# Down-weight loads of a 32-expert layer moved from SyncE's queue to ScalarE's

## The chip, the core and the metric

The kernel runs on one NeuronCore of one Trainium2 chip. The metric is the device time of one execution in microseconds. A profiled execution has a span, from its first to its last instruction; the device time is a little longer than the span. Names of engines in the rows: PE is TensorE (PEld its weight loads), DVE is VectorE, ACT is ScalarE, POOL is GpSimd, SP is SyncE. A "q" behind a name (SPq, ACTq) is the engine's sequencer when it issues a DMA.

## What is computed

One decoder layer for 256 tokens of width 1024: an attention mixer, a layer norm, a mixture of experts, a layer norm. Everything is float32. The change touches the mixture of experts only:

```python
def moe_ffn(h, ...):                      # 256 tokens, 32 experts, top 4
    logits = xt @ router_w + router_b
    top_logit, top_e = lax.top_k(logits, TOP_K)
    top_w = softmax(top_logit)
    # for each expert e, over the tokens xb that chose it, with weights w:
    gu = xb @ w_gu[e] + b_gu[e]           # 1024 x 2048: 8 MB of weights
    gate = minimum(gu[:, :1024], 7.0)
    up = clip(gu[:, 1024:], -7.0, 7.0)
    act = gate * sigmoid(1.702 * gate) * (up + 1.0)
    y = act @ w_dn[e] + b_dn[e]           # 1024 x 1024: 4 MB of weights
    out[tokens] += y * w
```

## The kernel before

The engines run five instruction streams, written by hand, and they order themselves with semaphores. The attention part and the router take the first 212 us of the span. After that come the 32 experts, in a rolled loop over 15 pairs (`Fori(0, PAIRS - 1)`) and a written-out last pair. An expert has 64 token slots; tokens beyond 64 go through `extra_blocks`, a conditional loop of 32-slot blocks behind the expert's down projection. In these inputs two experts have one extra block each, both with an odd number (experts 1 and 15).

Weights in SBUF. There are two gate-up slots of 8 MB (`gu_slot[0]`, `gu_slot[1]`), for even and odd experts, and one down slot of 4 MB (`dn_slot`). Each load is cut into four chunks: a gate-up chunk is 2 MB in 256 rows of 8 KB, a down chunk 1 MB in 256 rows of 4 KB. Every chunk has a semaphore of its own (`s_gul`, `s_dnl`), for which TensorE waits ahead of the chunk's matmuls.

TensorE's order (lines 1124 to 1170), for a pair of experts 2i and 2i+1: `combine` of the last pair, `gate_up(1)` for expert 2i+1, two `gather`s, `down(0)` for expert 2i, transposes, `gate_up(0)` for expert 2i+2, `down(1)` for expert 2i+1, transposes. So an expert's down projection stands behind the gate-up projection of the expert after it. A gate-up chunk increments `guc` when it has been used, a down chunk `dn_used`; chunks used by extra blocks increment `xguc` and `xdnc`.

SyncE's order (lines 368 to 389): for each expert e, first the four gate-up chunks of expert e+2, each as soon as the chunk that lies in its place has been used (waits on `guc` and `xguc`, lines 374 and 375), then the four down chunks of expert e+1, each as soon as the down chunk of e in its place has been used (waits on `dn_used` and `xdnc`, lines 379 and 380). All 256 expert loads are issued by SyncE, at line 325 (gate-up) and line 330 (down). They lie in its one DMA queue in this order, and SyncE stands still at each wait.

ScalarE's order (lines 685 to 705): for each expert a `sigmoid` (line 656), for every other one two copies of gathered tokens (`slots_to_sbuf`, line 622), then `expert_output` (line 672, the copy of half of the down result out of PSUM, behind all four `dn_used` of the expert), `extra_blocks`, and `act_columns` (line 660, the copy of the transposed activations that the next `down` multiplies; for even experts TensorE also waits for it, `actT`, ahead of the next `gate_up(1)`). `combine_weights` (line 667) ends the pair.

Of the kernel before, what the change touches and what calls it, by code (L numbers as in the profile page):

```python
# [13 lines left out]
P = 128  # L14
# [3 lines left out]
KT = D // P  # L18
DH = 64
CMP_LEN, CMP_STRIDE, CMP_BLOCKS = 32, 16, 16  # L20
N_EXPERTS = 32
TOP_K = 4
PAIRS = N_EXPERTS // 2
# [6 lines left out]
DN_CHUNKS = 4  # L30
# [24 lines left out]
def hybrid_layer(nc, x, w_in, b_in, pos_k, pos_v, w1_k, w2_k, w1_v, w2_v, g_out, w_out, ln1_g, ln1_b,  # L55
                 router_w, router_b, w_gu, b_gu, w_dn, b_dn, ln2_g, ln2_b, out):
    with ExitStack() as ctx:
# [3 lines left out]
        def sem(name):  # L61
            return ctx.enter_context(nc.semaphore(name))
# [6 lines left out]
        dn_slot = reg_dn.rearrange("p (k n) -> p k n", k=KT)  # L69
# [129 lines left out]
        sp = [take(768) for _ in range(2)]  # L199
# [30 lines left out]
        s = {n: sem("s_" + n) for n in names}  # L230
        s_win = [sem(f"s_win{i}") for i in range(5)]
        s_gul = [[sem(f"s_gul{e}{c}") for c in range(GU_CHUNKS)] for e in range(2)]
        s_dnl = [[sem(f"s_dnl{e}{c}") for c in range(DN_CHUNKS)] for e in range(2)]
# [55 lines left out]
        def _(sp_):  # L289
            sp = sp_  # L290
# [29 lines left out]
            dn_v = w_dn[0].rearrange("e (k p) n -> e p k n", p=P)  # L320

            def load_gu(i, par, c):
                kk = KT // GU_CHUNKS
                src = gu_v[2 * i + par] if isinstance(i, int) else gu_v[bass.ds(2 * i + par, 1)].rearrange("e p k n -> (e p) k n")
                sp.dma_start(gu_slot[par][:, kk * c:kk * c + kk, :], src[:, kk * c:kk * c + kk, :]).then_inc(s_gul[par][c], 16)  # L325

            def load_dn(i, par, c):
                kk = KT // DN_CHUNKS
                src = dn_v[2 * i + par] if isinstance(i, int) else dn_v[bass.ds(2 * i + par, 1)].rearrange("e p k n -> (e p) k n")
                sp.dma_start(dn_slot[:, kk * c:kk * c + kk, :], src[:, kk * c:kk * c + kk, :]).then_inc(s_dnl[par][c], 16)  # L330

            def count_extra_blocks(e):

                n = sp.value_load(nx[0:1, e:e + 1] if isinstance(e, int) else nx[0:1, bass.ds(e, 1)], min_val=0, max_val=MAX_EXTRA)  # L334
                sp.reg_add(xcount, xcount, n)

            def use_by_extra_blocks(c):

                return sp.snap(sp.snap(xcount, min_val=0, max_val=96) * 4 + (c + 1), min_val=1, max_val=4 * 97)
# [22 lines left out]
                load_gu(0, 1, c)  # L362
            sp.wait_ge(s["op"], 12)
            for c in range(DN_CHUNKS):
                load_dn(0, 0, c)
            sp.wait_ge(s["routed"], 1)

            with sp.Fori(0, PAIRS - 1) as i:
                for par in range(2):

                    count_extra_blocks(2 * i + par)
                    for c in range(GU_CHUNKS):
                        xc = use_by_extra_blocks(c)
                        sp.wait_ge(s["guc"], i * (2 * GU_CHUNKS) + (par * GU_CHUNKS + c + 1))
                        sp.wait_ge(s["xguc"], xc)
                        load_gu(i + 1, par, c)
                    for c in range(DN_CHUNKS):
                        xc = use_by_extra_blocks(c)
                        sp.wait_ge(s["dn_used"], i * (2 * DN_CHUNKS) + (par * DN_CHUNKS + c + 1))
                        sp.wait_ge(s["xdnc"], xc)  # L380
                        load_dn(i + par, 1 - par, c)

            count_extra_blocks(N_EXPERTS - 2)
            for c in range(DN_CHUNKS):
                xc = use_by_extra_blocks(c)
                sp.wait_ge(s["dn_used"], (N_EXPERTS - 2) * DN_CHUNKS + c + 1)
                sp.wait_ge(s["xdnc"], xc)
                load_dn(PAIRS - 1, 1, c)


            sp.wait_ge(s["guc"], (N_EXPERTS - 1) * GU_CHUNKS)
# [93 lines left out]
        def _(act):  # L485
# [134 lines left out]
            def slots_to_sbuf(h, bank, n):  # L620
                act.wait_ge(s["ga"], n)
                act.activation(xg[:, 4 * h:4 * h + 4, :].rearrange("p k s -> p (k s)"), PB[bank][:, :], ACT.Copy)\  # L622
                   .then_inc(s["xg_ok"], 1)
# [6 lines left out]
            def extra_slots():  # L630

                act.reg_add(xcount, xcount, 1)
                xc = act.snap(xcount, min_val=1, max_val=96)
                act.wait_ge(s["xga"], xc)
                act.activation(yx[:, 0:KT * XSLOTS], PB[6][:, 0:KT * XSLOTS], ACT.Copy).then_inc(s["xxg"], 1)

            def extra_sigmoid():
                act.wait_ge(s["xgok"], act.snap(xcount, min_val=1, max_val=96))
                act.activation(act_x[0:64, :], gt[0:64, :], ACT.Sigmoid, scale=SWIGLU_ALPHA).then_inc(s["xsig"], 1)

            def extra_act_copy():
                xc = act.snap(xcount, min_val=1, max_val=96)
                act.wait_ge(s["xct"], xc)
                act.activation(CTx[:, :, :].rearrange("p b t -> p (b t)"), PB[7][:, 0:256], ACT.Copy)\
                   .then_inc(s["xctd"], 1)
                act.wait_ge(s["xat"], xc)
                act.activation(actTx[:, :, :].rearrange("p c s -> p (c s)"), PB[6][:, 0:256], ACT.Copy)\
                   .then_inc(s["xactT"], 1)

            def extra_outputs():  # L650
                act.wait_ge(s["xdnc"], act.snap(act.snap(xcount, min_val=0, max_val=96) * 4 + DN_CHUNKS, min_val=1, max_val=4 * 97))
                act.activation(yx, PB[6][:, :], ACT.Copy).then_inc(s["xyd"], 1)

            def sigmoid(n):
                act.wait_ge(s["g_ok"], n)
                act.activation(act_sb, gt, ACT.Sigmoid, scale=SWIGLU_ALPHA).then_inc(s["sig"], 1)  # L656

            def act_columns(bank, n):
                act.wait_ge(s["at"], n)
                act.activation(actT[:, :, :].rearrange("p c s -> p (c s)"), PB[bank][:, :], ACT.Copy)\  # L660
                   .then_inc(s["actT"], 1)

            def combine_weights(n):

                act.wait_ge(s["ct"], n)
                act.wait_ge(s["comb"], n)
                act.activation(CT[:, :, :].rearrange("p b t -> p (b t)"), PB[6][:, 0:256], ACT.Copy)\
                   .then_inc(s["ct_sb"], 1)

            def expert_output(e, n):  # L670
                act.wait_ge(s["dn_used"], n * DN_CHUNKS)
                act.activation(ysb[64 * e:64 * e + 64, 1, :], PB[7][64:128, :], ACT.Copy).then_inc(s["ysb_ok"], 1)  # L672

            def extra_blocks(t):
                n = act.value_load(nx[0:1, t:t + 1] if isinstance(t, int) else nx[0:1, bass.ds(t, 1)], min_val=0,
                                   max_val=MAX_EXTRA)
                with act.If(n > 0):
                    with act.Fori(0, n):
                        extra_slots()
                        extra_sigmoid()  # L680
                        extra_act_copy()
                        extra_outputs()
                act.nop()

            sigmoid(1)
            act_columns(5, 1)
            combine_weights(1)
            with act.Fori(0, PAIRS - 1) as i:
                sigmoid(2 * i + 2)
                slots_to_sbuf(0, 6, 2 * i + 3)  # L690
                slots_to_sbuf(1, 4, 2 * i + 4)
                expert_output(0, 2 * i + 1)
                extra_blocks(2 * i)
                act_columns(6, 2 * i + 2)
                sigmoid(2 * i + 3)
                expert_output(1, 2 * i + 2)
                extra_blocks(2 * i + 1)
                act_columns(5, 2 * i + 3)
                combine_weights(i + 2)
            sigmoid(N_EXPERTS)  # L700
            expert_output(0, N_EXPERTS - 1)
            extra_blocks(N_EXPERTS - 2)
            act_columns(6, N_EXPERTS)
            expert_output(1, N_EXPERTS)
            extra_blocks(N_EXPERTS - 1)
# [461 lines left out]
        def _(dve):  # L1167
# [141 lines left out]
            def add_square(i):  # L1309
                kind, r = o_order[i]  # L1310
                if r > 0:
                    dve.wait_ge(s["oscaled"], i + 1)
                    a = ssq[:, {"nsa": 0, "fox": 1, "sb": 2}[kind], :]
                    tt(a, a, sq, ALU.add).then_inc(s["ssq_acc"], 1)
                    dve.wait_ge(s["ssq_acc"], sum(1 for _, q in o_order[:i + 1] if q > 0))
# [301 lines left out]
```

## Time and profile before

| | us |
|---|---|
| median of 3 runs | 1245.11 |
| lowest and highest | 1243.04 and 1245.42 |
| profiled execution, device time | 1245.07 |
| its span | 1243.3 |
| TensorE busy | 1115.8 |
| ScalarE busy | 146.3 |
| moved by the DMA engines | 426.18 MB |

The profiled execution's device time is 1.8 us above its span, and equal to the median within 0.04 us. The page divides the span into 40 slices of 31.1 us: slices 1 to 7 are attention and router, slice 8 on the experts. Times below are from the span's start. A busy time of TensorE is not a measure of its peak, since the ends of matmuls are modelled.

### The profile page before, as it was taken

Reading aid. Unit: us, or ns where it says so; the run is one execution under the profiler, and the core shown is the slowest. Engines: PE = TensorE matmul, PEld = TensorE weight load, DVE = VectorE, ACT = ScalarE, POOL = GpSimd, SP = SyncE. Lnnn points to the kernel's source line nnn. Section 1 sums busy time; section 2 is a strip of 40 time slices with the busy share of each in tenths; the row PEclk is TensorE's granted clock in tenths of the full one; section 3 lists DMA queues with packets and bytes.
Section 4 is the critical chain, followed back from the end, with each engine's and each line's share of the span. In section 5 each row is a group of like instructions: output and inputs, shape, how many; then the busy total and the mean of one; then the engine's idle time right before and its main releaser. Section 6 shows DMA issues by size and latency. Waiting matters only on the chain.

```text
span 1243.3 us, 14596 instructions
## 1 busy us (share of the span) xinstructions
PE 1115.8 (90%) x5388; PEld 489.2 (39%) x5389; DVE 266.8 (21%) x767; ACT 146.3 (12%) x309; POOL 29.7 (2%) x52
## 2 busy tenths in 40 slices
PE   7999796998899999999999978999999999999983
PEld 6677445334243333333333333434333332323321
DVE  2353535111112111120211111111212111111113
ACT  2043311100000110000100001000010010100000
POOL 2000410000000000000000000000000000000000
PEclk9999896997999999999999998999999999999997
DMA  9400849630999999999999957999999999999992
GB/s 315 180 1 1 269 196 395 273 137 2 408 418 418 418 418 418 419 418 418 418 418 418 418 243 314 418 418 418 418 418 418 418 419 418 418 418 418 418 414 119
DMA packets 80386, 426.18 MB, mean 343 GB/s; under 512 B 6009, under 2 KB 7594, under 8 KB 47562
## 3 DMA queue, kind: packets, MB, share of 16 engines
q1 hardware_dynamic: 79834, 425.37, 84.7%
q10 hardware_dynamic: 528, 0.48, 0.1%
q8 instruction: 16, 0.26, 0.1%
q14 instruction: 8, 0.07, 0.0%
HBM read 424.78 MB, written 1.05 MB: 343 GB/s over the span
## 4 chain that ended last, share of the span: by engine, by line
PE 49%; DMA 25%; SPq 18%; DVE 3%; issue 3%; ACT 1%; POOL 0%; DVEq 0%; POOLq 0%; ACTq 0%
PE PB L713 47%; DMA WB<-in_w_gate_up_dram 22%; SPq L330 11%; SPq L325 6%; DMA WB<-in_w_down_dram 3%; PE PB L1044 0%; DMA X<-in_x_dram 0%; SPq L334 0%; DVE S L1391 0%; PE PB L720 0%; DVE S L1520 0%; POOL K L476 0%; DVE WB L1285 0%; PE PB L803 0%; DVE S L1497 0%
## 5 line engine op out<-in xcount | busy, mean ns | idle before, releaser
L713 PE MATMUL PB<-WB,S 128*64 128x512 f32 (+5 forms) x3472 | 770.5, 596 | 60.6 <-DMA WB<-in_w_gate_up_dram 54.3
L713 PEld LDWEIGHTS PB<-WB,S 128*64 128x64 f32 (+2 forms) x3472 | 253.2, 140 | 541.7 <-issue 413.4
L1494 DVE TENSOR_SCALAR S<-PB 128x512 f32<-128x512 f32 (+1 forms) x34 | 23.5, 691 | 617.2 <-PE PB L713 617.2
L713 PE MATMUL PB<-S 128*64 128x512 f32 (+5 forms) x464 | 138.2, 580 | 4.7 <-issue 2.3
L656 ACT ACTIVATE S<-S 128x512 f32<-128x512 f32 x32 | 20.2, 630 | 568.7 <-DVE S L1494 568.7
L713 PE MATMUL PB<-S,X 128*128 128x128 f32 (+1 forms) x576 | 76.9, 295 | 9.3 <-DVE S L1520 8.0
L713 PEld LDWEIGHTS PB<-S,X 128*128 128x128 f32 x576 | 73.6, 211 | 23.7 <-issue 21.9
L713 PEld LDWEIGHTS PB<-S 128*64 128x64 f32 (+4 forms) x464 | 53.0, 167 | 74.4 <-issue 67.4
L1538 DVE COPY S<-PB 64x512 f32<-64x512 f32 x32 | 21.9, 684 | 197.6 <-PE PB L713 197.6
L713 PE MATMUL PB<-S,WB 128*128 128x256 f32 (+2 forms) x336 | 63.2, 388 | 0.4 <-ACT S L496 0.4
L713 PEld LDWEIGHTS PB<-S,WB 128*128 128x128 f32 (+1 forms) x336 | 49.1, 177 | 12.4 <-issue 2.1
L713 PE MATMUL PB<-WB 128*32 128x128 f32 (+7 forms) x260 | 44.6, 361 | 5.2 <-DVE WB L1358 3.3
L672 ACT ACTIVATE S<-PB 64x512 f32<-64x512 f32 x32 | 19.0, 594 | 194.9 <-PE PB L713 194.9
L713 PEld LDWEIGHTS PB<-WB 128*64 128x64 f32 (+2 forms) x260 | 27.4, 152 | 18.7 <-issue 13.7
L480 POOL TENSOR_TENSOR K<-K 128x1 f32<-128x1 f32 x2 | 3.0, 1512 | 1041.6 <-DVE K L1413 1041.6
L1044 PEld LDWEIGHTS PB<-K,S 128*128 128x128 f32 x128 | 13.4, 140 | 30.8 <-issue 27.0
L1044 PE MATMUL PB<-K,S 128*128 128x128 f32 x128 | 21.0, 287 | 4.8 <-DVE S L1500 2.8
L1497 DVE SCALAR_TENSOR_TENSOR S<-S 128x512 f32<-128x512 f32 (+1 forms) x34 | 23.5, 691 | 1.2
L1500 DVE TENSOR_TENSOR S<-S 128x512 f32<-128x512 f32 (+1 forms) x34 | 23.5, 691 | 1.2
L1495 DVE TENSOR_SCALAR S<-PB 128x512 f32<-128x512 f32 (+1 forms) x34 | 23.1, 681 | 0.1
L622 ACT ACTIVATE S<-PB 128x512 f32<-128x512 f32 x32 | 19.1, 597 | 32.9 <-PE PB L713 32.9
L1469 DVE TENSOR_SCALAR S<-K 128x64 f32<-128x64 f32 x68 | 16.9, 249 | 20.6 <-PE PB L1049 19.1
(198 smaller groups left out, 338.0 us busy)
## 6 DMA issues: line engine op xcount, KB each, us to landing
WB<-in_w_gate_up_dram SPq DMA_DIRECT2D x128, 2048.0 KB, 22.8
WB<-in_w_down_dram SPq DMA_DIRECT2D x128, 1024.0 KB, 22.9
WB<-in_w_in_dram SPq DMA_DIRECT2D x1, 3088.0 KB, 16.0
WB<-in_w_in_dram SPq DMA_DIRECT2D x1, 3072.0 KB, 20.7
WB<-in_w_in_dram SPq DMA_DIRECT2D x1, 2144.0 KB, 10.8
WB<-in_w_in_dram SPq DMA_DIRECT2D x1, 2048.0 KB, 15.8
WB<-in_w_out_dram SPq DMA_DIRECT2D x2, 1024.0 KB, 10.3
WB<-in_w_out_dram SPq DMA_DIRECT2D x1, 2048.0 KB, 16.8
```

The lines of the kernel that those rows point to most:

```text
L325: sp.dma_start(gu_slot[par][:, kk * c:kk * c + kk, :], src[:, kk * c:kk * c + kk, :]).then_inc(s_gul[par][c], 16)
L330: sp.dma_start(dn_slot[:, kk * c:kk * c + kk, :], src[:, kk * c:kk * c + kk, :]).then_inc(s_dnl[par][c], 16)
L622: act.activation(xg[:, 4 * h:4 * h + 4, :].rearrange("p k s -> p (k s)"), PB[bank][:, :], ACT.Copy)\
L656: act.activation(act_sb, gt, ACT.Sigmoid, scale=SWIGLU_ALPHA).then_inc(s["sig"], 1)
L672: act.activation(ysb[64 * e:64 * e + 64, 1, :], PB[7][64:128, :], ACT.Copy).then_inc(s["ysb_ok"], 1)
L713: return mm_(o, l, r, start=start, stop=stop, skip_group_check=True)
L1044: ins = tr(PB[bank][:, P * c:P * c + P], act_sb[:, P * c:P * c + P], ident)
L1494: ts(g, gate, LIMIT, None, ALU.min).then_inc(s[g_ok], 1)
L1495: ts(u, up, LIMIT, -LIMIT, ALU.min, ALU.max).then_inc(s[clip], 1)
L1497: stt(u, u, 1.0, g, ALU.add, ALU.mult).then_inc(s[upg], 1)
L1500: tt(a, u, a, ALU.mult).then_inc(s[done], 1)
L1538: cp(ysb[64 * e:64 * e + 64, 0, :], PB[7][0:64, :]).then_inc(s["ysb_dv"], 1)
```

## The change

SyncE issues only the first expert's down weights and all gate-up weights. The four down chunks of every later expert are issued by ScalarE, together, behind `expert_output` and `extra_blocks` of the expert before, and so behind the waits for all of that expert's down chunks; the waits on `dn_used` and `xdnc` chunk by chunk are gone. In ScalarE's stream `act_columns` comes behind the four issues. SyncE's gate-up loads keep their waits on `guc` and `xguc` and their order.

```diff
-            def load_dn(i, par, c):
+            def load_first_dn(c):
                 kk = KT // DN_CHUNKS
-                src = dn_v[2 * i + par] if isinstance(i, int) else ...
-                sp.dma_start(dn_slot[:, kk * c:kk * c + kk, :], src[...]).then_inc(s_dnl[par][c], 16)
+                sp.dma_start(dn_slot[:, kk * c:kk * c + kk, :], dn_v[0, :, kk * c:kk * c + kk, :]).then_inc(s_dnl[0][c], 16)
...
                         load_gu(i + 1, par, c)
-                    for c in range(DN_CHUNKS):
-                        xc = use_by_extra_blocks(c)
-                        sp.wait_ge(s["dn_used"], i * (2 * DN_CHUNKS) + (par * DN_CHUNKS + c + 1))
-                        sp.wait_ge(s["xdnc"], xc)
-                        load_dn(i + par, 1 - par, c)
...
+            def load_dn(t, par):
+                kk = KT // DN_CHUNKS
+                src = dn_v[t] if isinstance(t, int) else dn_v[bass.ds(t, 1)].rearrange("e p k n -> (e p) k n")
+                for c in range(DN_CHUNKS):
+                    act.dma_start(dn_slot[:, kk * c:kk * c + kk, :], src[:, kk * c:kk * c + kk, :]).then_inc(s_dnl[par][c], 16)
...
                 expert_output(0, 2 * i + 1)
                 extra_blocks(2 * i)
+                load_dn(2 * i + 1, 1)
                 act_columns(6, 2 * i + 2)
                 sigmoid(2 * i + 3)
                 expert_output(1, 2 * i + 2)
                 extra_blocks(2 * i + 1)
+                load_dn(2 * i + 2, 0)
                 act_columns(5, 2 * i + 3)
                 combine_weights(i + 2)
...
             extra_blocks(N_EXPERTS - 2)
+            load_dn(N_EXPERTS - 1, 1)
             act_columns(6, N_EXPERTS)
```

## Rows read from the trace of the kernel before

**Rows 1.** The page, part 2: granted TensorE clock and GB/s in 40 slices

```profile
PEclk9999896997999999999999998999999999999997
GB/s 315 180 1 1 269 196 395 273 137 2 408 418 418 418 418 418 419 418 418 418 418 418 418 243 314 418 418 418 418 418 418 418 419 418 418 418 418 418 414 119
```

**Rows 2.** The chain that ended last, by engine, and one piece of it

```profile
PE 49%; DMA 25%; SPq 18%; DVE 3%; issue 3%; ACT 1%; POOL 0%; DVEq 0%; POOLq 0%; ACTq 0%
...
456.01 27.93 DMA WB<-in_w_gate_up_dram
```

**Rows 3.** Stretches: us, busy PE PEld DVE ACT POOL (instructions), PEclk, DMA share, GB/s

```profile
329.80:382.60 52.80, 52.80 (x253) 19.92 (x251) 8.07 (x19) 4.40 (x8) 0.00 (x0) 1.00 1.02 417
...
442.00:502.00 60.00, 55.28 (x262) 20.50 (x260) 9.47 (x24) 5.22 (x9) 0.00 (x0) 1.00 1.02 418
...
329.20:737.10 407.90, 381.71 (x1806) 142.62 (x1803) 64.90 (x163) 35.96 (x62) 0.00 (x0) 1.00 1.01 414
...
770.00:1178.00 408.00, 381.69 (x1808) 142.96 (x1806) 64.89 (x163) 35.95 (x62) 0.00 (x0) 1.00 1.02 418
```

**Rows 4.** DMA issues by line: count, KB each, median us to landing

```profile
WB<-in_w_gate_up_dram SPq DMA_DIRECT2D x128, 2048.0 KB, 22.8
WB<-in_w_down_dram SPq DMA_DIRECT2D x128, 1024.0 KB, 22.9
```

**Rows 5.** Waits: engine, line, waited for: total us, times, longest

```profile
SPq L380 <- PE PB L713: 256.9, 85, 29.4
...
PE PB L713 <- DMA WB<-in_w_gate_up_dram: 54.3, 42, 1.4
...
PE PB L713 <- DMA WB<-in_w_down_dram: 2.1, 4, 0.6
```

**Rows 6.** Timeline of PE over one pair: start, us, line, operation

```profile
329.59 3.60 PE L713 MATMUL PB<-S 128*128 128x512 f32 x8
333.12 13.95 PE L713 MATMUL PB<-WB,S 128*64 128x512 f32 x64
...
352.49 7.09 PE L713 MATMUL PB<-WB,S 128*64 128x512 f32 x32
359.51 0.66 PE L1044 MATMUL PB<-K,S 128*128 128x128 f32 x4
...
375.60 7.04 PE L713 MATMUL PB<-WB,S 128*64 128x512 f32 x32
382.57 0.66 PE L1044 MATMUL PB<-K,S 128*128 128x128 f32 x4
383.06 0.38 PE L1049 MATMUL PB<-K,S 128*128 128x128 f32 x2
```

**Rows 7.** DMA packets by queue, 192.2 to 194.6 us (q1 SyncE's, q10 ScalarE's)

```profile
q1 hardware_dynamic: 40, 0.33, 61.2%
q10 hardware_dynamic: 38, 0.26, 41.5%
```

**Rows 8.** Expert loads of the whole span: issue to landing

```profile
DMA to landing us min/median/max: 5.0/22.8/27.9
```

**Rows 9.** Timeline around ScalarE's copies, and one of its own DMA issues

```profile
204.93 0.32 ACTq L614 DMA_DIRECT2D S<-in_b_down_dram x1
...
530.31 0.60 ACT L672 ACTIVATE S<-PB 64x512 f32<-64x512 f32 x1 [6.43 <-PE PB L713]
531.11 0.60 ACT L660 ACTIVATE S<-PB 128x512 f32<-128x512 f32 x1 [0.21 <-PE PB L1044]
```

**Rows 10.** Timeline of SyncE's queue in the steady part: four down chunks issued

```profile
491.33 15.20 SPq L330 DMA_DIRECT2D WB<-in_w_down_dram  x4
```

**Rows 11.** Around the extra block of expert 15: PE's timeline, then stretches as in rows 3

```profile
741.14 6.84 PE L713 MATMUL PB<-S,X 128*128 128x32 f32 x32 [3.98 <-DVE S L1520]
...
741.00:748.00 7.00, 6.84 (x32) 6.74 (x32) 0.00 (x0) 0.00 (x0) 0.00 (x0) 0.52 0.00 0
...
737.00:752.00 15.00, 10.54 (x54) 7.65 (x56) 3.21 (x14) 0.98 (x2) 0.00 (x0) 0.66 0.00 0
```

**Rows 12.** The last two down projections: stretches as in rows 3

```profile
1178.30:1207.90 29.60, 26.07 (x112) 8.52 (x110) 5.71 (x17) 2.20 (x4) 0.00 (x0) 1.00 1.02 415
1207.90:1220.10 12.20, 10.09 (x44) 2.85 (x44) 0.68 (x1) 1.19 (x2) 0.00 (x0) 1.00 0.91 359
```

More of the change, by code:

```diff
@@ L325, in load_gu @@
                 sp.dma_start(gu_slot[par][:, kk * c:kk * c + kk, :], src[:, kk * c:kk * c + kk, :]).then_inc(s_gul[par][c], 16)
-            def load_dn(i, par, c):
+            def load_first_dn(c):
                 kk = KT // DN_CHUNKS
-                src = dn_v[2 * i + par] if isinstance(i, int) else dn_v[bass.ds(2 * i + par, 1)].rearrange("e p k n -> (e p) k n")
-                sp.dma_start(dn_slot[:, kk * c:kk * c + kk, :], src[:, kk * c:kk * c + kk, :]).then_inc(s_dnl[par][c], 16)
+                sp.dma_start(dn_slot[:, kk * c:kk * c + kk, :], dn_v[0, :, kk * c:kk * c + kk, :]).then_inc(s_dnl[0][c], 16)
             def count_extra_blocks(e):
@@ L364, in _ @@
             for c in range(DN_CHUNKS):
-                load_dn(0, 0, c)
+                load_first_dn(c)
             sp.wait_ge(s["routed"], 1)
@@ L376, in _ @@
                         load_gu(i + 1, par, c)
-                    for c in range(DN_CHUNKS):
-                        xc = use_by_extra_blocks(c)
-                        sp.wait_ge(s["dn_used"], i * (2 * DN_CHUNKS) + (par * DN_CHUNKS + c + 1))
-                        sp.wait_ge(s["xdnc"], xc)
-                        load_dn(i + par, 1 - par, c)
-            count_extra_blocks(N_EXPERTS - 2)
[L384 to L388, printed above, removed]
+            count_extra_blocks(N_EXPERTS - 2)
             sp.wait_ge(s["guc"], (N_EXPERTS - 1) * GU_CHUNKS)
@@ L683, in extra_blocks @@
                 act.nop()
+            dn_v = w_dn[0].rearrange("e (k p) n -> e p k n", p=P)
+            def load_dn(t, par):
[3 more added lines that the diff above has]
+                    act.dma_start(dn_slot[:, kk * c:kk * c + kk, :], src[:, kk * c:kk * c + kk, :]).then_inc(s_dnl[par][c], 16)
             sigmoid(1)
```

## The prediction

> **What bounds the kernel now.** I read the page's slices first. From the eleventh slice on the DMA engines move 408 to 419 GB/s in every slice but the two around the extra block of expert 15 and the last two [rows 1]. The chain of waits gives TensorE 49%, DMA 25% and SyncE's queue 18% [rows 2]; the last two shares are one thing, a loaded queue, since the chain's pieces there are issues held back behind transfers, or a transfer such as the one of 27.93 us. The stretches say which engine ends last [rows 3]. From 329.8 to 382.6 us TensorE is busy for all of 52.80 us: it bounds. From 442 to 502 us it is busy for 55.28 of 60.00 us while the DMA rate is the same 418 GB/s: the transfers bound.
>
> Two floors of a pair of experts follow. Transfers: 8 gate-up chunks of 2048 KB and 8 down chunks of 1024 KB [rows 4] are 25.2 MB, at 418 GB/s 60.2 us (a gate-up chunk 5.0 us, a down chunk 2.5 us; per expert 20.1 and 10.0 us). TensorE: from the combine at 329.59 to the next one behind the transposes at 383.06 + 0.38 it is 53.8 us [rows 6]. Seven pairs lie between the two extra blocks in 407.9 us and seven behind the second in 408.0 us, 58.3 us a pair [rows 3]: the first are near TensorE's floor, working off what had been loaded ahead, the rest at the transfers' 60.2.
>
> The waits view must not mislead. SyncE waits 256.9 us for down chunks to be used [rows 5], and the gate-up loads queue behind that. But while it waits, its DMA queue is full: a load takes a median 22.8 us to land, and at least 5.0 us [rows 4, 8]. TensorE waits 54.3 us for gate-up weights, never over 1.4 us at a time, and 2.1 us for down weights [rows 5]. So the order in the one queue delivers each chunk about when it is needed, and the wait at SyncE costs nothing in the loaded stretches.
>
> **The change part by part.** (1) Taken from SyncE: 124 issues and their waits. Gate-up chunks can be issued earlier by the time SyncE stood at down waits. In loaded stretches that adds no bytes per second. In the two stops the DMA engines do fall dry (0 GB/s from 737 to 752 us [rows 11]), but there the gate-up loads wait for `xguc`, the extra block's own use of the slot, which stays. I cost the gain at nothing.
>
> (2) Added to ScalarE: 31 times four issues. The nearest rows: one issue of its own took 0.32 us, and behind the output copy at 530.31 the next copy started at 531.11 [rows 9]. I take 0.8 us from the end of `down` to the first issue and some 0.45 us for each, 1.8 us. The copy of the activations is late by that. For the next `down` it has a whole gate-up projection as cover; for `gate_up(1)` it has the combine, 3.6 us, plus 1.0 us of transposes ahead of it [rows 6]. So 1.8 us is hidden, if ScalarE's sequencer isn't held. If it is, see the third rival.
>
> (3) The down load itself starts later. Before, each chunk was issued when its place was free, 5.1 us from first to last. Now all four start behind the whole `down`. From `down`'s end to the first data it is 0.8 us to the issue, and the 5.0 us least landing less 2.5 us of transfer [rows 8], together 3.3 us; the last chunk's matmuls take 7.1 / 4 = 1.8 us [rows 6].
>
> (4) The two queues share the DMA engines. This decides. The only place where the trace shows both loaded is ScalarE's bias load at 192 us: 40 packets of SyncE's queue beside 38 of ScalarE's, 0.33 and 0.26 MB [rows 7]. The engines take packets in turn, one of each. There both were of 8 KB; a down chunk has rows of 4 KB and a gate-up chunk rows of 8 KB. If a turn is a row, down weights get one byte in three while gate-up loads are queued, and their 10.0 us become 30.1 us. The two bounds are 10.0 us (down weights served first) and 30.1 us; I take 30.1 us, the reading that is nearest to rows 7.
>
> The Trainium skill has this ("DMA: Bandwidth & Descriptors", Queues, rings and completion order): an engine goes round its queues and drains a packet from each before switching. The trace agrees for equal rows. The same page (SWDGE vs HWDGE vs iDMA) gives a packet as preferably no more than 4096 B. By that the turns would be of equal bytes, which is the first rival.
>
> (5) What a pair then takes. From one `down`'s end to the next with gate-up loads queued all the time: 3.3 + 30.1 + 1.8 = 35.2 us. TensorE's own time between the same points is 382.57 − 359.51 = 23.1 us for odd experts and 53.8 − 23.1 = 30.7 us for even ones [rows 6]. So odd experts' down weights are late by up to 12 us and even ones' by up to 4.5 us. Gate-up loads aren't queued all the time, however: in two such intervals they could move 2 × (30.1 × 2/3 + 5.1) = 50 us worth and a pair needs 40.1. They fill their slots, stop, and the down load gets the whole rate for a while. I give that relief to the even expert, which comes back to TensorE's 30.7 us: 35.2 + 30.7 = 65.9 us a pair. The other end is the transfers' 60.2 us. Above 60.2 the DMA engines fall dry for part of the pair, with both slots full and no down load issued, and this in turn speeds the next down load, so the pair settles between: I take the middle, 63.1 us.
>
> Sum: 14 pairs × 63.1 − (407.9 + 408.0) = 883.4 − 815.9 = **+67.5 us**. At the ends: 60.2 gives +27, 65.9 gives +107.
>
> (6) TensorE's clock. A wait of 3.98 us ahead of 741.14 us is followed by a stretch with a granted clock of 0.52 of 2.4 GHz, so 1.2 GHz nearly throughout, until past 748 us [rows 11]. The new waits for down chunks are of some 5 us each, so the last chunk's matmuls may take 3.5 instead of 1.8 us and the start of the next gate-up projection is slow too. Bounds 0 and 14 × 1.8 = 25 us; most lies beside waiting, so I take +5 us.
>
> (7) The tail. Before, from 1178.3 us, 29.6 + 12.2 = 41.8 us [rows 12]. After: combine 3.6, gate-up 15.6, down 7.1 and transposes 0.7, then 3.3 + 10.0 + 1.8 = 15.1 us for the last down weights, which no gate-up load shares: 42.1 us. I take 0. Before 329 us nothing is late: the load of expert 1's down weights has an empty queue and over 20 us.
>
> Total: 1245.1 + 67.5 + 5 = 1317.6; I say **1317 us**, 72 us slower. The sum is made against the profiled execution's 1245.07 us, which is the median.
>
> **The rivals.** *Turns of equal bytes.* Then a shared down load takes 20.1 us: 3.3 + 20.1 + 1.8 = 25.2 us against 23.1 and 30.7, 55.9 us a pair, under 60.2. Only the pairs that TensorE bounds today, some three in each half, lose 2.1 us each (13 us), and the stops and the tail some 4 us for loads that start later: 1262 us. For it: the skill's packet size. Against it: rows 7 count packets, and none there is split. Its own range is 1254 to 1275.
>
> *The freed gate-up queue fills dry time* (the other side). If gate-up loads could run while the DMA engines now stand dry, 737 to 752 us and a few us around it, 17 us of the loaded stretch behind it would be saved: 1228 us. It decides from the point at which a gate-up load is ready while SyncE stands at a down wait and its queue is dry. The `xguc` wait speaks against it in both stops.
>
> *ScalarE is held at its issues.* SyncE's four down issues take 15.20 us when its queue is loaded [rows 10]. If the room for issued rows is shared by both queues, ScalarE stands for as long, its activation copy comes 0.8 + 15.2 us behind `down`, the combine covers 4.6 us, and even intervals grow by 11.4 us: a pair is then between 30.7 + 11.4 + 23.1 = 65.2 and 77.3 us, 1342 to 1511 us, with 1427 in the middle. Against it: ScalarE's queue never holds more than four chunks, and its own issue took 0.32 us with SyncE's queue in use [rows 9].
>
> *Down weights served first.* Their load takes 10.0 us, nothing is late, and only the later start of (3) costs: 1245 to 1254 us.
>
> **How the numbers follow.** The forecast, 1275 to 1342 us: 0.63. Turns of equal bytes: 0.15. ScalarE held: 0.12. Down weights first: 0.04, of which 0.01 is within 0.2%. Dry time filled: 0.05. Nothing of all that happens and the time stays: 0.01. The range is 1256 to 1362 us: it leaves out the filled dry time, the unchanged time, down weights first and some two thirds of the third rival, 0.18. Faster by over 0.2% 0.05, within 0.2% 0.02, slower by over 0.2% 0.93; 0.2% is about what a measurement of this kernel can tell.
>
> **What would show it.** Down chunks issued by ScalarE land some 10 us after issue for the first and 30 us for the fourth where gate-up loads are queued; TensorE's waits for down weights grow from 2.1 us to over 100 us in total, and those for gate-up weights all but vanish; slices show less than 418 GB/s; pairs repeat at 60 to 66 us. ScalarE's four issues take about 0.4 us each, and the activation copy comes within 3 us. The prediction is wrong if in a window with both queues loaded ScalarE's queue moves half of the bytes or more, or if its issues take microseconds.

## The result and the profile after

| | before | after |
|---|---|---|
| device time, median us | 1244.07 | 1313.88 |
| lowest and highest, 4 runs each | 1242.36 and 1245.42 | 1308.61 and 1320.04 |
| profiled execution: device time, span | 1245.07, 1243.3 | 1308.61, 1306.8 |

The ratio is 1.057, with a 95% interval of 1.054 to 1.060: the change makes the kernel 70 us slower. The forecast was 1317 us. The profiled execution of after is the fastest of its four, so differences read from the two traces add up to 63.5 us, not 70. In the experiments one execution stood apart: of the thirteen of the kernel with the later start alone, one, the profiled one, took 2336.24 us; its ratio leaves it out, and no row of its trace is read.

The page of after, part 2: granted clock, share of the DMA engines and GB/s in 40 slices of 32.7 us.

```profile
PEclk9999897897988899899899979989899979998997
DMA  9300958435999999999999519999999999999742
GB/s 320 151 1 19 339 212 329 180 130 228 418 418 419 393 419 418 401 404 418 418 387 407 214 67 420 420 419 416 417 397 419 419 381 407 419 418 390 304 171 119
```

Against [rows 1] the ceiling is the same, 418 to 420 GB/s, but it no longer holds all the time: 393, 401, 387, 397, 381 stand in slices that nothing but experts fills, and the clock has dropped in many of them. The same 426.18 MB are moved.

The waits of TensorE in after (engine, line, waited for: total us, times, longest), then the issues with their median us to landing.

```profile
PE PB L714 <- DMA WB<-in_w_down_dram: 96.4, 30, 5.6
PE PB L714 <- DVE S L1521: 8.0, 2, 4.0
```

```profile
WB<-in_w_gate_up_dram SPq DMA_DIRECT2D x128, 2048.0 KB, 16.0
WB<-in_w_down_dram ACTq DMA_DIRECT2D x124, 1024.0 KB, 11.9
```

Compare [rows 5]: the 54.3 us of waits for gate-up weights are gone from the list, and 2.1 us for down weights have become 96.4 us. Gate-up weights are now early (they land in a median 16.0 us, before 22.8 us [rows 4]), down weights late. Their median landing of 11.9 us looks better than the 22.9 us of before, and misleads: a load that starts late may land soon and still be too late.

**One late down load, read through.** ScalarE's timeline behind expert 2's down projection (start, us, line, operation, in brackets the idle time before it).

```profile
360.94 0.59 ACT L661 ACTIVATE S<-PB 64x512 f32<-64x512 f32 x1 [9.84 <-PE PB L714]
361.86 2.00 ACTq L681 DMA_DIRECT2D WB<-in_w_down_dram  x4
363.90 0.60 ACT L649 ACTIVATE S<-PB 128x512 f32<-128x512 f32 x1 [2.36 <-issue]
```

The same four issues, asked one by one: KB and us from issue to landing.

```profile
WB<-in_w_down_dram ACTq DMA_DIRECT2D x1, 1024.0 KB, 11.6
WB<-in_w_down_dram ACTq DMA_DIRECT2D x1, 1024.0 KB, 18.6
WB<-in_w_down_dram ACTq DMA_DIRECT2D x1, 1024.0 KB, 25.6
WB<-in_w_down_dram ACTq DMA_DIRECT2D x1, 1024.0 KB, 32.6
```

The issues follow each other by 0.54 us and the landings by 7.5 us (7.0 + 0.54). A down chunk alone takes 2.5 us, so the down load runs at a third of the rate. TensorE, in the same time:

```profile
375.20 1.89 PE L714 MATMUL PB<-S 128*64 128x512 f32 x8
376.91 1.89 PE L714 MATMUL PB<-WB,S 128*64 128x512 f32 x8
381.08 3.30 PE L714 MATMUL PB<-WB,S 128*64 128x512 f32 x8 [2.28 <-DMA WB<-in_w_down_dram]
388.62 3.48 PE L714 MATMUL PB<-WB,S 128*64 128x512 f32 x8 [4.24 <-DMA WB<-in_w_down_dram]
396.17 3.68 PE L714 MATMUL PB<-WB,S 128*64 128x512 f32 x8 [4.07 <-DMA WB<-in_w_down_dram]
```

Its gate-up projection ends at 377 us, and three of the four down chunks are waited for. Their matmuls take 3.30 to 3.68 us where the first chunk's take 1.89: the granted clock is 1.00 of 2.4 GHz from 375 to 379 us, and 0.58, 0.55 and 0.50 in the stretches of the three. The last of them, columns as in [rows 3]:

```profile
396.10:399.80 3.70, 3.63 (x9) 0.79 (x9) 0.00 (x0) 0.00 (x0) 0.00 (x0) 0.50 1.01 421
```

The chain that ended last, over this stretch, by line:

```profile
by line: DMA WB<-in_w_down_dram 79.6%; PE PB L714 9.0%; ACTq L681 6.7%; issue 2.7%; ACTq L664 2.2%; ACTq L666 0.2%; ACT S L661 0.1%
```

A down load is released by ScalarE, lands, and lets `down` end, which releases the next. And it isn't for want of transfers that it is late: packets by queue from 362 to 400 us (packets, MB, share of the engines), at 418 GB/s in sum.

```profile
q1 hardware_dynamic: 1523, 11.70, 73.9%
q10 hardware_dynamic: 1088, 4.19, 27.6%
```

In these 38 us the gate-up queue moved 11.70 MB that TensorE couldn't use yet, while it waited for 4.19 MB in the other. These packets don't show the turns, since the down load fills only part of the 38 us. From 375 to 385 us both queues are loaded all the time:

```profile
q1 hardware_dynamic: 356, 2.79, 66.9%
q10 hardware_dynamic: 357, 1.40, 34.9%
```

As many packets from one queue as from the other, nearly every packet being one row, and so twice as many bytes of gate-up weights.

**Where the time went.** The stretches of seven pairs, as in [rows 3], and the stop behind the first of them:

```profile
327.20:764.30 437.10, 393.42 (x1805) 147.85 (x1803) 64.93 (x163) 35.95 (x62) 0.00 (x0) 0.95 0.94 386
799.10:1241.30 442.20, 394.16 (x1805) 147.05 (x1803) 64.93 (x163) 35.95 (x62) 0.00 (x0) 0.95 0.99 403
764.30:784.00 19.70, 15.24 (x90) 9.03 (x92) 3.21 (x14) 0.98 (x2) 0.00 (x0) 0.65 0.17 55
```

437.1 + 442.2 − 407.9 − 408.0 = 63.4 us, all of the difference. A pair takes 62.8 us in the mean; before it was 58.3. From one pair's weight transposes to the next pair's (L1049, after L1050) the full pairs of the first stretch took 53.7, 54.0, 59.6, 60.2, 60.2 and 60.2 us before, and take 73.4, 63.1, 67.2, 56.0, 67.9 and 55.8 us after: from the third on they alternate between some 67 and 56. The rest cancels: the time ahead of 327 us is 2 us less, the stop between the stretches 1.4 us more, the tail 0.6 us more.

### The profile page after: what moved, and what is told of

Read it like the earlier page. It is cut to its first block, busy times and chain, and to the rows that moved or that the text cites. A ratio compares the mean times of both kernels' runs of the same rounds, so it can differ in the third digit from the quotient of the medians.

```text
span 1306.8 us, 14351 instructions
## 1 busy us (share of the span) xinstructions
PE 1142.2 (87%) x5388; PEld 500.8 (38%) x5389; DVE 266.9 (20%) x767; ACT 146.3 (11%) x309; POOL 29.6 (2%) x52
## 2 busy tenths in 40 slices
DMA packets 80386, 426.18 MB, mean 326 GB/s; under 512 B 6009, under 2 KB 7594, under 8 KB 47562
## 4 chain that ended last, share of the span: by engine, by line
PE 47%; DMA 43%; DVE 3%; ACTq 3%; issue 2%; ACT 1%; SPq 0%; POOL 0%; DVEq 0%; POOLq 0%
PE PB L714 45%; DMA WB<-in_w_down_dram 42%; ACTq L681 2%; DMA WB<-in_w_in_dram 1%; ACTq L664 1%; PE PB L1045 1%; DVE S L1392 0%; DVE S L1521 0%; POOL K L465 0%; SPq L304 0%; DVE WB L1286 0%; PE PB L1050 0%; PE PB L804 0%; DVE S L1498 0%; DVE S L1501 0%
## 5 line engine op out<-in xcount | busy, mean ns | idle before, releaser
L714 PE MATMUL PB<-WB,S 128*64 128x512 f32 (+5 forms) x3472 | 792.0, 612 | 99.8 <-DMA WB<-in_w_down_dram 96.4
L714 PEld LDWEIGHTS PB<-WB,S 128*64 128x64 f32 (+2 forms) x3472 | 261.3, 143 | 587.3 <-issue 456.0
L714 PE MATMUL PB<-S 128*64 128x512 f32 (+5 forms) x464 | 141.4, 588 | 4.3 <-issue 2.3
L661 ACT ACTIVATE S<-PB 64x512 f32<-64x512 f32 x32 | 19.0, 594 | 318.3 <-PE PB L714 318.3
L649 ACT ACTIVATE S<-PB 128x512 f32<-128x512 f32 x32 | 19.1, 597 | 79.6 <-issue 71.7
L1045 PE MATMUL PB<-K,S 128*128 128x128 f32 x128 | 24.0, 317 | 2.9 <-DVE S L1501 2.8
L611 ACT ACTIVATE S<-PB 128x512 f32<-128x512 f32 x32 | 19.1, 597 | 33.0 <-PE PB L714 33.0
## 6 DMA issues: line engine op xcount, KB each, us to landing
WB<-in_w_down_dram ACTq DMA_DIRECT2D x124, 1024.0 KB, 11.9
WB<-in_w_in_dram SPq DMA_DIRECT2D x1, 3088.0 KB, 16.1
```

The costliest lines, as they stand in the source:

```text
L714: return mm_(o, l, r, start=start, stop=stop, skip_group_check=True)
L1045: ins = tr(PB[bank][:, P * c:P * c + P], act_sb[:, P * c:P * c + P], ident)
```

## The experiments

Theory A: the DMA engines serve the two queues in turn, row by row, so down rows of 4 KB beside gate-up rows of 8 KB get a third of the bytes, and that is nearly all of the loss. Theory B: the loss comes from the down loads' later start and from ScalarE's place in their path. Each experiment was timed beside the kernel before; its median is given with the ratio to those runs.

**Cutting the gate-up rows, two queues and one.** The first kernel changes the length of a row, and with it the number of issues; the second is its control with one queue.

```diff
-                sp.dma_start(gu_slot[par][:, kk * c:kk * c + kk, :], src[:, kk * c:kk * c + kk, :]).then_inc(s_gul[par][c], 16)
+                for h in range(2):
+                    sp.dma_start(gu_slot[par][:, kk * c:kk * c + kk, 1024 * h:1024 * h + 1024],
+                                 src[:, kk * c:kk * c + kk, 1024 * h:1024 * h + 1024]).then_inc(s_gul[par][c], 16)
...
-                    pe.wait_ge(s_gul[e][c], 16 * loaded)
+                    pe.wait_ge(s_gul[e][c], 32 * loaded)
```

> The changed kernel, with each gate-up chunk loaded as two halves of 1024 columns, so that its rows are 4 KB like the down rows; bytes, order and waits unchanged. Theory A (the queues take turns row by row): turns are now of equal bytes, a down chunk that shares the engines lands every 5.0 us instead of every 7.5 us, waits for down weights shrink from 96 us to under 45 us, and the time falls to about 1262 us (1250 to 1275). Theory B (the loss comes from the down loads' later start and from ScalarE in their path, not from the share): nothing about that is changed, 1305 to 1320 us.

> The control for the run above: the kernel before, all loads in SyncE's queue, with the gate-up chunks in halves of 4 KB rows. With one queue there are no turns, so theory A says as before, 1244 us, plus at most 10 us if 4 KB rows or twice as many issues cost anything. Theory B says the same. If this run is slower than 1254 us, the run above has to be read against it.

Measured: two queues 1276.35 us (1.026, 1.023 to 1.029), one queue 1263.49 us (1.017, 1.014 to 1.020). Waits for down weights fell to 49.7 us. The landings of four down chunks, issued 0.54 us apart, are now 5.1 us apart instead of 7.5:

```profile
WB<-in_w_down_dram ACTq DMA_DIRECT2D x1, 1024.0 KB, 9.4
WB<-in_w_down_dram ACTq DMA_DIRECT2D x1, 1024.0 KB, 14.0
WB<-in_w_down_dram ACTq DMA_DIRECT2D x1, 1024.0 KB, 18.6
WB<-in_w_down_dram ACTq DMA_DIRECT2D x1, 1024.0 KB, 23.2
```

Both times are above what was expected, for the same reason: halves of the 8 KB rows are moved at 410 GB/s, not 418. The stretch from 500 to 700 us of the one-queue control (columns of rows 3):

```profile
500.00:700.00 200.00, 179.56 (x830) 65.00 (x828) 30.38 (x82) 16.07 (x28) 0.00 (x0) 1.00 1.03 410
```

Against its control the split now costs 13 us, not 70. Theory B would have left it at 70: the later start and ScalarE's place are the same here.

**Quarters.** The same edit with four pieces of 512 columns: rows of 2 KB.

> The changed kernel, each gate-up chunk loaded as four quarters of 512 columns, rows of 2 KB against the down loads' 4 KB. Theory A: down weights now get two bytes in three while both queues are loaded, a shared down chunk lands every 3.8 us, a whole down load in some 18 us from issue, TensorE waits for down weights nearly nowhere but at the last expert, and the time is 1245 to 1275 us, unless 2 KB rows lower the 418 GB/s. Theory B: 1305 to 1320 us.

Measured: 1318.72 us (1.060, 1.058 to 1.063), 44 us above the range. The time alone would speak for theory B. The profile doesn't: TensorE's longest entry is another one, its waits for down weights are three, and the stretch from 500 to 700 us has a lower rate.

```profile
PE PB L716 <- DMA WB<-in_w_gate_up_dram: 106.5, 20, 8.6
PE PB L716 <- DMA WB<-in_w_down_dram: 5.8, 3, 5.3
```

```profile
500.00:700.00 200.00, 177.56 (x816) 66.25 (x814) 28.42 (x72) 15.67 (x27) 0.00 (x0) 0.94 1.04 394
```

Down weights land 3.9 us apart, as expected, and TensorE waits 5.8 us in all for them. Now gate-up weights are late, and at 394 GB/s a pair's 25.2 MB take 63.9 us, 5.6 us above the 58.3 of before; 14 pairs are 78 us, against 75 measured. The condition that I had put into the expectation (unless 2 KB rows lower the rate) is what happened. The kernel with one queue and quarters was not run, so how much the split costs at this ratio isn't known. Cut rows mix two effects, so the later kernels, from the whole rows on, avoid cutting.

**The later start alone.** One queue; SyncE waits for the whole of `down` before it issues the four down chunks.

```diff
-                        xc = use_by_extra_blocks(c)
-                        sp.wait_ge(s["dn_used"], i * (2 * DN_CHUNKS) + (par * DN_CHUNKS + c + 1))
-                        sp.wait_ge(s["xdnc"], xc)
+                        if c == 0:
+                            xc = use_by_extra_blocks(DN_CHUNKS - 1)
+                            sp.wait_ge(s["dn_used"], i * (2 * DN_CHUNKS) + (par * DN_CHUNKS + DN_CHUNKS))
+                            sp.wait_ge(s["xdnc"], xc)
                         load_dn(i + par, 1 - par, c)
...
```

> The kernel before with one part of the change alone: SyncE still issues the down loads in its one queue, but all four chunks together behind the whole down projection (and extra block) of the expert before, instead of chunk by chunk. Theory A: the queue is loaded in the steady part, so a start 5 us later costs nothing there and some 3 us at the last expert: 1244 to 1252 us. Theory B: the later start is most of the loss, 1290 us or more.

Measured: 1247.02 us (1.0026, 1.0010 to 1.0042). With one queue the start 5 us later costs 3 us of the 70, so the start alone isn't the loss. It says nothing of ScalarE's place, the other half of theory B, nor of a late start beside a second queue; against these speak the kernels in which both stay and the loss is 13 to 20 us.

**Down rows of 2 KB.** The other way round: the share made worse, with the same bytes.

```diff
-                    act.dma_start(dn_slot[:, kk * c:kk * c + kk, :], src[:, kk * c:kk * c + kk, :]).then_inc(s_dnl[par][c], 16)
+                    for h in range(2):
+                        act.dma_start(dn_slot[:, kk * c:kk * c + kk, 512 * h:512 * h + 512],
+                                      src[:, kk * c:kk * c + kk, 512 * h:512 * h + 512]).then_inc(s_dnl[par][c], 16)
...
```

> The changed kernel, each down chunk loaded as two halves of 512 columns, so that its rows are 2 KB against the gate-up loads' 8 KB. Theory A (the queues take turns row by row) predicts a large loss from a change that moves no more bytes: down weights get one byte in five while gate-up loads are queued, their shared chunks land every 12.5 us or a little more, a pair takes up to 70 us, and the time is 1376 us (1340 to 1410). A rival (turns of equal bytes, or by whole loads): 1308 to 1325 us as with the change.

Measured: 1456.89 us (1.172, 1.167 to 1.177), 81 us above the expected value and 47 above the range. The waits say in part why:

```profile
PE PB L718 <- DMA WB<-in_w_down_dram: 193.3, 31, 10.7
PE PB L718 <- ACT S L651: 30.2, 15, 7.7
```

The first line is the share. From 337 to 347 us, with both queues loaded, the packets are again as many in one as in the other:

```profile
q1 hardware_dynamic: 441, 3.35, 80.5%
q10 hardware_dynamic: 441, 0.84, 22.1%
```

The second is ScalarE held at its issues. Eight of them take 4.1 to 4.6 us where none is held, and up to 13.5 us where some are, as here:

```profile
874.05 13.19 ACTq L684 DMA_DIRECT2D WB<-in_w_down_dram  x8
```

Its copy of the activations then comes so late that the combine no longer covers it, 15 times, 2.0 us in the mean and 7.7 at most. SyncE's queue doesn't cause this: in the kernel with halves above, three of ScalarE's issues took 1.45 us together, the second and third while one of SyncE's was held for 4.14 us.

```profile
359.88 1.45 ACTq L683 DMA_DIRECT2D WB<-in_w_down_dram  x3
360.10 4.14 SPq L326 DMA_DIRECT2D WB<-in_w_gate_up_dram  x1
```

The remaining excess was not taken apart.

**Whole rows of equal length.** Now the row length is changed without cutting. The contraction index of the down projection may be dealt to partitions in any order, as long as the activations follow: partition p reads the two neighbouring rows 2p and 2p + 1 of a block of 256, one run of 8 KB, and the transposes pick every second column.

```diff
-            dn_v = w_dn[0].rearrange("e (k p) n -> e p k n", p=P)
+            dn_v = w_dn[0].rearrange("e (c p q) n -> e p c (q n)", p=P, q=2)
...
-                    act.dma_start(dn_slot[:, kk * c:kk * c + kk, :], src[:, kk * c:kk * c + kk, :]).then_inc(s_dnl[par][c], 16)
+                    act.dma_start(reg_dn[:, 2 * D * c:2 * D * c + 2 * D], src[:, c, :]).then_inc(s_dnl[par][c], 16)
...
-                    ins = tr(PB[bank][:, P * c:P * c + P], act_sb[:, P * c:P * c + P], ident)
+                    a0 = 256 * (c // 2) + c % 2
+                    ins = tr(PB[bank][:, P * c:P * c + P], act_sb[:, a0:a0 + 255:2], ident)
...
```

> The changed kernel, with the down weights of a chunk laid so that a partition reads two neighbouring rows of the matrix in one run of 8 KB (the transposes of the activations pick every second column to match). Rows of both queues are 8 KB, none is cut. Theory A: turns of equal bytes at the full 418 GB/s, a shared down chunk lands every 5.0 us, 1257 us (1250 to 1265), 13 to 18 us above its one-queue control. Its rival, that cutting gate-up rows helped in another way: 1300 to 1320 us.

> The control for the run above: the kernel before, one queue, with the same 8 KB runs for the down weights. One queue has no turns, so 1244 us, or up to 4 us less, since 8 KB rows load slightly faster than 4 KB rows (4 chunks in 20.0 us for 8 MB against 10.1 us for 4 MB).

Measured: two queues 1255.68 us (1.011, 1.008 to 1.014), one queue 1235.64 us (0.994, 0.992 to 0.996). The first is in its range; the loss against the control is 20 us, 2 us above what was expected. The control is 4 us below its range: one queue with whole rows of 8 KB is faster than the kernel before. In the two-queue kernel the fourth down chunk lands 23.0 us after its issue, instead of 32.6:

```profile
WB<-in_w_down_dram ACTq DMA_DIRECT2D x1, 1024.0 KB, 23.0
```

**Longer rows everywhere, one queue.** The same for the gate-up weights, with rows of 16 KB, added to the control above.

```diff
-            gu_v = w_gu[0].rearrange("e (k p) n -> e p k n", p=P)
+            gu_v = w_gu[0].rearrange("e (c p q) n -> e p c (q n)", p=P, q=2)
...
-                        ins = mm(PB[bank][:, P * k:P * k + P], x_sb[:, b, P * (4 * h + k):P * (4 * h + k) + P],
+                        x0 = 256 * (2 * h + k // 2) + k % 2
+                        ins = mm(PB[bank][:, P * k:P * k + P], x_sb[:, b, x0:x0 + 255:2],
...
```

> A candidate to beat both kernels: the kernel before, with runs of 8 KB for down weights and of 16 KB for gate-up weights (the gathers pick every second column to match). If part of a row's time is fixed, as 418, 410 and 393 GB/s for three row sizes suggest, the rate rises above 418 GB/s in the loaded stretches, by up to 2%, and the time falls to 1228 to 1240 us. If the rate is at its ceiling: 1244 us.

Measured: 1226.76 us (0.987, 0.985 to 0.990), 1 us below the range and faster than both kernels. Its steady part, then that of the kernel before:

```profile
500.00:700.00 200.00, 186.24 (x884) 71.57 (x882) 31.07 (x76) 17.49 (x30) 0.00 (x0) 1.00 1.01 426
```

```profile
500.00:700.00 200.00, 181.31 (x848) 65.51 (x846) 28.42 (x72) 16.05 (x28) 0.00 (x0) 1.00 1.02 418
```

426 instead of 418 GB/s, while the bytes are the same: where transfers bound, 2% of rate is 2% of time (the later pairs of a stretch take 59.0 us, before 60.2).

**The ratio, or the length?** Two queues with these longer rows, 16 KB and 8 KB: the ratio of before, other lengths.

> Two queues again, with the long runs of the fastest kernel so far: gate-up rows of 16 KB, down rows of 8 KB. The down rows are as long as in e6_dn8k_after, where 12 to 20 us were lost; only the ratio is back at two to one. Theory A (what counts is the ratio of the row lengths): shared down chunks land every 7.4 us again and the loss against the one-queue kernel with the same rows (1227 us) is again about 65 to 75 us: 1297 us (1288 to 1305). A rival (short down rows of 4 KB were the trouble): the loss is 20 us as in e6_dn8k_after, 1247 us.

Measured: 1294.20 us (1.041, 1.035 to 1.046), 67 us above its one-queue kernel. The last down chunks of a shared load, issued 0.5 us apart, land 7.4 us apart again, as expected (the third and the fourth):

```profile
WB<-in_w_down_dram ACTq DMA_DIRECT2D x1, 1024.0 KB, 19.4
WB<-in_w_down_dram ACTq DMA_DIRECT2D x1, 1024.0 KB, 26.3
```

The down rows are as long as where 20 us were lost. The ratio decides.

**The ratio turned round.** Gate-up rows 8 KB, down rows 16 KB (`q=4`, two pieces of 2 MB, TensorE waits ahead of chunks 0 and 2).

> Two queues, the ratio turned round without cutting a row: gate-up rows of 8 KB, down rows of 16 KB (a down load is then two pieces of 2 MB; the transposes pick every fourth column). Theory A: down weights get two bytes in three, both pieces have landed some 19 us from their issue, down is on time for TensorE's 23.1 us, and as no row is cut the 418 GB/s hold, unlike in e3_gu2k_after: 1238 to 1252 us, waits now for gate-up weights. A rival (any two loaded queues cost some tens of us, as e3_gu2k_after had it): 1290 us or more.

> The control for the run above: one queue, down rows of 16 KB in two pieces of 2 MB, each issued when its half of the slot has been used. Theory A: as e7_dn8k_before or a little less, 1228 to 1238 us, so that two queues with down weights favoured still lose some 10 us to one queue, through the later start and the last expert.

Measured: two queues 1248.48 us (1.004, 1.002 to 1.007), one queue 1230.75 us (0.991, 0.987 to 0.994). The two pieces, issued 0.49 us apart, land 7.4 us apart, so 3.7 us for each MB. TensorE's waits in the two-queue kernel:

```profile
PE PB L714 <- DMA WB<-in_w_gate_up_dram: 42.0, 8, 6.8
PE PB L714 <- DMA WB<-in_w_down_dram: 13.5, 14, 7.7
```

Both times are in their ranges. With two queues even this ratio leaves 18 us lost. The two sums of waits don't explain it, since the control waits nearly as long (32.7 us for gate-up weights, 16.1 us for down weights).

All the ratios together. The last column is two queues less one queue, with the same rows.

| gate-up row, down row | bytes for down in a shared time | two queues, us | one queue, us | loss, us |
|---|---|---|---|---|
| 8 KB, 2 KB pieces | 1/5 | 1456.89 | not run | |
| 8 KB, 4 KB (the change) | 1/3 | 1313.88 | 1244.07 | 70 |
| 16 KB, 8 KB | 1/3 | 1294.20 | 1226.76 | 67 |
| 4 KB pieces, 4 KB | 1/2 | 1276.35 | 1263.49 | 13 |
| 8 KB, 8 KB | 1/2 | 1255.68 | 1235.64 | 20 |
| 8 KB, 16 KB | 2/3 | 1248.48 | 1230.75 | 18 |
| 2 KB pieces, 4 KB | 2/3 | 1318.72 | not run | |

What the good ratios still lose shows in the pairs, measured from one pair's weight transposes to the next pair's. With rows of 8 KB in both and one queue the first two pairs of each stretch take 53.9 and 54.1 us, TensorE's own time, with weights that had been loaded ahead, and the last ones 59.6 or 59.7 us. With two queues they take 58.3 to 60.8 us from the first on: a shared down load takes 24.5 us from its first issue to its last landing, and TensorE has 23.1 us for an odd expert. That is 28 us more in thirteen pairs; the two pairs with an extra block take 11 us less, for which I have no account. With down rows of 16 KB, pairs of 54.6 to 54.8 us and of 62.6 to 64.3 us alternate nearly throughout: down weights are there in time, gate-up weights in every second pair are not. Their mean is that of the control's later pairs (59.3 us), so here too the loss lies outside the steady pairs; it was not taken apart further.

## Why the prediction was right

**What bounds.** The floors were read rightly: transfers where 418 GB/s hold, TensorE elsewhere (two pairs of each stretch, where the first rival counted three). The wait of 256.9 us at SyncE for down chunks was called free, and nothing speaks against it: in after SyncE waits only for gate-up chunks to be used, gate-up weights come early, and no gain shows. What the freed wait would be worth without the loss wasn't measured.

**Step 1, nothing gained in the dry time.** Right. From 764.3 to 784.0 us the engines move 55 GB/s in the mean; the `xguc` wait holds the gate-up loads as before. That the dry time could be filled without this wait was not tried.

**Step 2, ScalarE's issues.** I had 0.8 us to the first and 1.8 us for four; it was 361.86 − 360.82 = 1.0 us and 2.0 us. The activations' copy ends the later for it, and yet no entry for ScalarE of more than 1.4 us stands in TensorE's waits. With eight issues the cover was used up, so it was small.

**Step 3, the later start.** 3.3 + 1.8 us by the prediction. The start alone costs 3 us with one queue. With two it is part of a closed chain, and some of the 13 to 20 us that good ratios leave may be its share; how much wasn't separated.

**Step 4, the share.** This decided, and it held in each ratio: chunks 7.5, 5.1 and 3.9 us apart for rows of 8, 4 and 2 KB beside 4 KB, and as many packets from either queue where both are loaded. By the sign named for being wrong, half of the bytes or more in ScalarE's queue, it is 1.40 of 4.19 MB, a third. The Trainium skill's preferred packet of 4096 B ("DMA: Bandwidth & Descriptors", SWDGE vs HWDGE vs iDMA) would have given turns of equal bytes and 1262 us; the trace does not agree with it for these rows, and the first rival fell with it. Its other rule on the same page (Queues, rings and completion order), that an engine drains a packet of a queue and then turns to the next, agrees with the landings and the packet counts if a packet is one row, of 2 to 16 KB.

**Step 5, the pair.** 63.1 us predicted, 62.8 measured; +67.5 us predicted, +63.4 in the trace. The number was right and one assumption behind it wasn't. I had every odd expert late, with 35.2 us, and every even one relieved to 30.7. ScalarE's output copies (L661) show the intervals instead: from one `down` end to the next, in the first stretch 68.5 (with the extra block), 39.0, 38.7, 24.8, 33.4, 33.4, 31.4, 25.0, 32.5, 35.3, 30.9, 25.0, 30.9, 23.1 us. The intervals are those of experts 2 to 15. The even ones come near TensorE's 30.7 only from expert 8 on (30.9 to 32.5); of the odd ones every second is relieved too, to about 25 us, and the others take 33 to 39. So pairs of about 56 and 67 us alternate, and their mean comes out where I had put each. The gate-up loads run ahead, stop, and let one down load through at the full rate; then it begins again. A single late interval is longer than 35.2: 1.0 + 1.6 us until the last issue, 32.6 us to its landing and 3.7 us for its matmuls are 38.9 us, of which 1.9 us are the clock and 1.6 us a first landing that comes later under load (11.6 us) than 2.5 us and a shared chunk of 7.5 make. Taking the middle between the two ends was luck in part: it had no argument but that the time must lie between. TensorE's waits for down weights came to 96.4 us, just short of the 100 named as a sign.

**Step 6, the clock.** +5 us predicted, within 0 and 25. The same matmuls are busy for 393.42 + 394.16 us instead of 381.71 + 381.69 us, 24.2 us more, at a mean granted clock of 0.95 instead of 1.00. The 25 us of the bound were all but reached; how much of it lies on the path and how much beside a wait wasn't separated, so whether 5 us were right stays open.

**Step 7, the tail.** 42.1 us predicted, 1283.6 − 1241.2 = 42.4 us in the trace.

**The other rivals.** ScalarE held at its issues: the four took 2.0 us. In after none of SyncE's issues is held at such a moment, so this trace alone doesn't settle whether room is shared; the kernel with halves does, where ScalarE's issues went out beside a held one of SyncE's. With eight pieces in its own queue ScalarE was held, so the cost that the rival names is real, and what kept it away was that ScalarE's queue holds four chunks at most. (Of the 15.20 us of [rows 10] some 2 us are waits for chunks to be used and not issues, so 15.2 us was too much for it.) Down weights first: not seen. Faster: nothing in that direction; each two-queue kernel that has a one-queue control lost against it, by 13 to 70 us.

## What to carry to other kernels

An order in one queue is a schedule: here it delivered each load about when it was due, and the waits in it cost nothing that shows while the queue ahead was full. Put two streams on two queues and the engines divide them by rows, not by need, so before a split work out the share from the row lengths and ask which stream is due first. Where transfers bound, lengthen the rows by dealing the contraction index in neighbouring pairs (16.0 us here, 1242.78 − 1226.76, from 16 KB and 8 KB runs, with strided reads on TensorE's side, where the pairs that it bounds took 54.1 instead of 53.7 us), and don't cut them.

## What the runs showed of the hardware

- Two loaded queues get one row each in turn, in each pair of row lengths tried, between 2 and 16 KB: 1 MB of down weights in rows of 4 KB took 7.5, 5.1 and 3.9 us beside rows of 8, 4 and 2 KB, and 3.7 us in rows of 16 KB beside 8 KB; in 10 us the two queues had 356 and 357 packets (8 KB beside 4 KB) and 441 and 441 (8 KB beside 2 KB).
- The rate depends on the rows: with one queue 426 GB/s for gate-up and down rows of 16 and 8 KB, 424 for 8 and 16 KB, 422 for 8 and 8 KB, 418 for 8 and 4 KB and 410 with the 8 KB rows in halves; with two queues and quarters 394. I had expected at most 10 us from halves; it was 19.
- A first chunk of 1 MB in the second queue lands 11.6 us after its issue beside a first queue loaded with rows of 8 KB, and 4.9 us at the last expert of after, where no gate-up load is left.
- The room for issued rows is each queue's own: with halves two of ScalarE's issues took 0.38 us each while one of SyncE's was held for 4.14 us. It isn't counted in bytes: with one queue SyncE's gate-up issues of 2 MB took a median 2.06 us with rows of 8 KB and 0.33 us with rows of 16 KB, though the loads then landed a median 30.1 us after their issue, not 22.8.
- Behind waits of 2.28, 4.24 and 4.07 us the granted clock of TensorE in a down chunk was 0.58, 0.55 and 0.50 of 2.4 GHz, the last of them 1.2 GHz throughout: the chunk took 3.30 to 3.68 us instead of 1.89.
